# Latent attention: probabilities scaled before the transpose and split in two parts, values applied to two query tiles at once, residual rows parked in memory

## The chip, the cores and the metric

One core of a Trainium2 chip runs the whole program. The metric is the device time of one execution in microseconds; a profiled execution gives the trace.

## What is computed

Two transformer layers on 1024 tokens of width 1024, with mixers, a state space model, MLPs and, in the second layer, causal latent attention. The change is in that attention: 8 heads, query and key of 128 + 64 elements, values of 128.

```python
s = (q_nope @ k_nope.T + q_rope @ k_rope.T) * SM_SCALE      # per head, 1024 x 1024, float32
p = softmax(where(key <= query, s, -1e30))
o = p @ v                                                  # v = latent @ w, 128 wide
x = x + concat(o) @ w_o                                    # then layer norm and MLP
```

## The kernel before

Matrices that need float32 accuracy are held as a high and a low part of a shorter float format (`F32R`, a `Pair`); `mm3` multiplies such pairs with three instructions. Five engines run queues of their own, in an order written out by hand, tied by semaphores: TensorE (PE, `pe`) multiplies and transposes, VectorE (DVE, `dve`), ScalarE (ACT, `act`) and GpSimd (POOL) calculate, SyncE (SP) issues DMAs. TensorE writes PSUM, eight banks of 128x512.

`stage_attention` loops over heads `h`. A head starts with projections: `rope` in two halves, `nope`, `folded`, and in even heads `value_tiles`, which projects the values of two heads in four banks; `value_copy` brings them to SBUF in full float32. Then comes a loop over eight query tiles `t` of 128 rows. Tile `t` has `t+1` blocks of 128 keys (causal). In round `t` TensorE transposes the tile's exponentials (L3557), computes `scores` of tile `t+2` (in rounds 6 and 7 `keys` of the next head, in the last head `product.begin`, the first steps of the output product), transposes the finished rows of tile `t-1` (`turn_rows`, L3523) and multiplies the transposed exponentials with the values (L3580, full float32, two instructions a block). VectorE takes the maximum (L3665) and its negative (L3667), the reciprocal of the sum (L3701), scales the result rows (`scaled_rows`, L3672), copies part of the transposed exponentials (L3704) and makes the low part of the result (`low_part`, L3678). ScalarE makes exponentials with their sum (`expo`, L3608), copies the other part (L3626) and the high part of the result (L3613). The scaling by 1/sum stands behind the product with the values.

The order of VectorE in round `t`:

```python
if t: scaled_rows(h, t - 1)
# reciprocal(t); copy of blocks 4.. of tile t
if t + 2 < NT: maximum(h, t + 2)
if t == 0: rope_low(h, 1)
if t: low_part(h, t - 1)
```

Behind attention `Product` multiplies with the output weights: two passes over eight tiles at 256 columns, one at 512. Its weights come in four chunks over one raw buffer: SP loads chunk n when n-1 is split, GpSimd splits it (L289, L294). Chunk 1 may load once all heads are done. VectorE adds each result to the residual rows `x` (L1471), which lie in SBUF at 64 to 96 KB per partition throughout. TensorE's second pass waits for chunk 1's split and for the additions of the first.

## Time and profile before

| | us |
|---|---|
| median of 3 runs | 3170.9 (3167.88 to 3170.93) |
| the profiled execution | 3169.23, span 3167.4 |
| busy in the span: PE, DVE, ACT, POOL | 3096.3, 2017.4, 1063.0, 1410.4 |
| mean granted TensorE clock | 0.995 of full |
| attention stage, about | 2055 to 2395 |

Busy times are sums over the span; PE's matmuls overlap, so that its pace is read from their starts. A round's order on each engine is read from the timeline, and who waits for whom from the list of waits.

### The profile page before, as it was taken

What the parts mean: (1) busy time and instruction counts of PE and PEld (TensorE: products, weight loads), DVE (VectorE), ACT (ScalarE), POOL (GpSimd) and SP (SyncE); (2) the same over time, 40 slices, a digit from 0 to 9 for tenths busy, and PEclk for the clock granted to TensorE, in tenths of its full rate; (3) what the DMA queues carried; (4) which work ended last, traced back from release to release, by engine and by line L of the source; (5) the groups of instructions that cost most, each with busy time, mean ns of one, the idle gap of its engine ahead of it and who ended that gap; (6) DMA issues with size and microseconds to landing.
All of it is one profiled execution on the core that took longest, in us unless ns stands there. A gap on an engine that the chain in (4) does not pass through costs nothing.

```text
span 3167.4 us, 48769 instructions
## 1 busy us (share of the span) xinstructions
PE 3096.3 (98%) x17764; PEld 2629.3 (83%) x17764; DVE 2017.4 (64%) x3766; ACT 1063.0 (34%) x2061; POOL 1410.4 (45%) x1203
## 2 busy tenths in 40 slices
PE   9999999999999999999999999999999999999998
PEld 8787778788987889888888888988889788888886
DVE  4757576655898212777777775555553777777766
ACT  3546464631133210422222222544341422222221
POOL 5534343326544324755555545311114755555533
PEclk9999999999999999999999999999999999999999
DMA  7211111052212112011111111000002011111111
GB/s 204 75 53 53 53 53 52 14 203 82 71 29 57 53 53 94 27 54 53 46 46 53 53 40 64 11 17 18 17 21 94 28 53 53 53 53 53 53 53 53
DMA packets 181816, 179.39 MB, mean 57 GB/s; under 512 B 50234, under 2 KB 163066, under 8 KB 181498
## 3 DMA queue, kind: packets, MB, share of 16 engines
q1 hardware_dynamic: 181566, 177.02, 17.5%
q8 instruction: 104, 1.70, 0.2%
q14 instruction: 50, 0.41, 0.0%
q10 hardware_dynamic: 96, 0.26, 0.0%
HBM read 160.12 MB, written 22.38 MB: 58 GB/s over the span
## 4 chain that ended last, share of the span: by engine, by line
PE 63%; DVE 2%; issue 1%; ACT 1%; POOL 0%; POOLq 0%; DVEq 0%; ACTq 0%
PE banks L2763 17%; PE banks L79 14%; PE banks L81 14%; PE banks L80 14%; PE banks L3580 2%; PE banks L3557 1%; PE banks L215 1%; PE banks L3514 0%; PE banks L3515 0%; PE banks L3496 0%; POOL x L183 0%; PE banks L3523 0%; PE banks L2385 0%; DVE x L3000 0%; POOL rstd L178 0%
## 5 line engine op out<-in xcount | busy, mean ns | idle before, releaser
L3000 DVE TENSOR_TENSOR x<-x,banks 128x512 f32<-128x512 f32 x784 | 523.2, 687 | 241.4 <-PE banks L2763 232.9
L79 PE MATMUL banks<-winhi,xt_hi 128*128 128x512 f32 (+1 forms) x576 | 224.5, 390 | 8.4 <-ACT vz L990 3.8
L81 PE MATMUL banks<-winhi,xt_lo 128*128 128x512 f32 (+1 forms) x576 | 212.3, 369 | 0.0
L80 PE MATMUL banks<-winlo,xt_hi 128*128 128x512 f32 (+1 forms) x576 | 211.9, 368 | 0.0
L79 PE MATMUL banks<-h1t_hi,f1w_buf_hi 128*128 128x512 f32 x512 | 199.5, 390 | 1.6 <-issue 1.6
L79 PE MATMUL banks<-h3t_hi,f2w_buf_hi 128*128 128x512 f32 x512 | 199.5, 390 | 1.6 <-issue 1.6
L81 PE MATMUL banks<-h1t_hi,f1w_buf_lo 128*128 128x512 f32 x512 | 199.2, 389 | 0.0
L81 PE MATMUL banks<-h3t_hi,f2w_buf_lo 128*128 128x512 f32 x512 | 199.2, 389 | 0.0
L80 PE MATMUL banks<-h1t_lo,f1w_buf_hi 128*128 128x512 f32 x512 | 199.2, 389 | 0.0
L80 PE MATMUL banks<-h3t_lo,f2w_buf_hi 128*128 128x512 f32 x512 | 199.2, 389 | 0.0
L1013 ACT ACTIVATE scores<-scores,mixsmall 128x1024 f32<-128x1024 f32 (+2 forms) x128 | 122.8, 960 | 90.6 <-DVE mixsmall L1189 90.4
L633 POOL TENSOR_TENSOR mixsmall<-mixsmall,neghalf 128x4 f32<-128x4 f32 x64 | 66.3, 1035 | 190.2 <-DVE mixsmall L1152 190.1
L79 PEld LDWEIGHTS banks<-winhi,xt_hi 128*128 128x128 f32 x576 | 109.3, 190 | 43.9 <-issue 16.5
L81 PEld LDWEIGHTS banks<-winhi,xt_lo 128*128 128x128 f32 x576 | 109.2, 190 | 18.6
L80 PEld LDWEIGHTS banks<-winlo,xt_hi 128*128 128x128 f32 x576 | 109.5, 190 | 14.2
L79 PEld LDWEIGHTS banks<-h3t_hi,f2w_buf_hi 128*128 128x128 f32 x512 | 96.1, 188 | 21.7 <-issue 1.8
L79 PEld LDWEIGHTS banks<-h1t_hi,f1w_buf_hi 128*128 128x128 f32 x512 | 96.1, 188 | 21.6 <-issue 1.8
L81 PEld LDWEIGHTS banks<-h1t_hi,f1w_buf_lo 128*128 128x128 f32 x512 | 96.1, 188 | 20.0
L81 PEld LDWEIGHTS banks<-h3t_hi,f2w_buf_lo 128*128 128x128 f32 x512 | 96.1, 188 | 20.0
L80 PEld LDWEIGHTS banks<-h1t_lo,f1w_buf_hi 128*128 128x128 f32 x512 | 96.1, 188 | 19.9
L80 PEld LDWEIGHTS banks<-h3t_lo,f2w_buf_hi 128*128 128x128 f32 x512 | 96.1, 188 | 19.9
L2565 POOL TENSOR_TENSOR f1w_terms_lo<-f1w_raw,f1w_terms_hi 128x512 fp32r<-128x512 f32 x42 | 54.9, 1309 | 126.7 <-ACT f1w_terms_hi L2561 125.1
(552 smaller groups left out, 9327.2 us busy)
## 6 DMA issues: line engine op xcount, KB each, us to landing
f1w_raw<-in_w_ff SPq DMA_DIRECT2D x32, 1024.0 KB, 5.0
f2w_raw<-in_w_ff SPq DMA_DIRECT2D x32, 1024.0 KB, 5.1
winraw<-in_w_in SPq DMA_DIRECT2D x128, 128.0 KB, 2.4
gluw_raw<-in_ssm_w_glu SPq DMA_DIRECT2D x14, 512.0 KB, 4.6
x<-in_x SPq DMA_DIRECT2D x8, 512.0 KB, 6.4
wow_raw<-in_w_out SPq DMA_DIRECT2D x4, 1024.0 KB, 5.9
x<-in_x SPq DMA_DIRECT2D x1, 4096.0 KB, 14.8
gew_raw<-in_w_ple_gate SPq DMA_DIRECT2D x4, 1024.0 KB, 5.0
```

Source lines behind the costliest of these rows:

```text
L79: nc.tensor.matmul(out, a.hi, b.hi, start=start, stop=False)
L80: nc.tensor.matmul(out, a.hi, b.lo, start=False, stop=False)
L81: return nc.tensor.matmul(out, a.lo, b.hi, start=False, stop=stop)
L215: last = self.nc.tensor.transpose(self.bank(j, q)[:, k * P:(k + 1) * P], self.x[:, j, (4 * q + k) * P:(4 * q + k + 1) * P], self.chip.iden ...
L633: nc.gpsimd.tensor_tensor(m.rq[:, a % 2, :], m.ss4[:, a % 2, :], chip.neghalf[:, 0:1].to_broadcast([P, 4]), ALU.pow).then_inc(s_rp, 1)
L1013: nc.scalar.activation(m.s[:, g % 2, c, 0:w], m.s[:, g % 2, c, 0:w], ACT.Exp, bias=m.mx[:, g % 2, c:c + 1], accum_out=m.z[:, g % 2, c:c + ...
L2565: self.nc.gpsimd.tensor_tensor(self.terms.lo[:, k, :], self.source(k), f32(self.terms.hi[:, k, :]), ALU.subtract).then_inc(self.split, 1)
L2763: last = nc.tensor.matmul(chip.ps[:, 4 + 2 * (p % 2) + g, :], left, right, start=i == 0 and p in (0, 1, 3), stop=i == 2, skip_group_check= ...
L3000: nc.vector.tensor_tensor(xx, xx, chip.ps[:, 4 + 2 * (p % 2) + g, :], ALU.add).then_inc(s_acc, 1)
L3557: last = nc.tensor.transpose(chip.ps[:, 4 + n // 4, (n % 4) * P:(n % 4 + 1) * P], s[:, t % 2, n * P:(n + 1) * P], chip.ident[:, :])
L3580: last = nc.tensor.matmul(chip.ps[:, 6 + t % 2, 0:P], pt[:, t % 2, n * P:(n + 1) * P], v[:, n, h % 2, :], start=n == 0, stop=n == t)
```

## The change

Rows of exponentials are scaled by 1/sum in place in SBUF (`scaled_rows`, which now holds the reciprocal too) before TensorE transposes them (`turn`), in pieces of up to four blocks. ScalarE copies each piece as the high part (`turned_high`), VectorE subtracts for the low part (`turned_low`). The transposed parts of two tiles lie side by side in `pt`, and `pair_values` multiplies them with values that are split as well (`value_high`, `value_low`), with three instructions a block at 256 columns, half a pair in a round; pair 3 of a head is done within the next head, in its rounds 0 and 1 if the head before was even, between the two `rope` halves if it was odd, and behind `product.begin(pe, 2)` after the last. Its result comes out already transposed, so `turn_rows` goes; `pair_high` and `pair_low` split it. `pt` grows to 28 KB and takes the place of residual rows 0 to 6, which SP stores to memory when they are final and loads back at the end: rows 0 to 2 once pair 2 of the last head is done, 3 to 6 after pair 3, ahead of the output weights' chunk 1.

```diff
         self.nc, self.chip, self.ws, self.rows, self.x, self.x_scale, self.norm = nc, chip, ws, rows, x, x_scale, norm
-        self.ready, self.begun = ready, 0
+        self.ready, self.begun, self.rows_back = ready, 0, [None] * NT
...
             n, j = u // NT, u % NT
+            if n == 0 and self.rows_back[j] is not None:
+                dve.wait_ge(*self.rows_back[j])
...
-def stage_attention(nc, block, chip, io, latent, heads, ot, product):
+def stage_attention(nc, block, chip, io, latent, heads, ot, product, x, x_norm):
...
     with ExitStack() as ctx:
...
         qrt = chip.at("qrt", 32, [P, SEQ], F32R)
-        v = chip.at("v", 36, [P, NT, 2, VH])
+        v = Pair(chip.at("v_hi", 36, [P, NT, 2, VH], F32R), chip.at("v_lo", 52, [P, NT, 2, VH], F32R))
...
         s = chip.at("s", 44, [P, 2, SEQ])
-        pt = chip.at("pt", 52, [P, 2, SEQ])
+        pt = chip.at("pt", 64, [P, 14, 2, 2 * P], F32R)
+        AWAY, FREE = 7, 3
...
         ident_r = chip.at("ident_r", 61.5, [P, P], F32R)
-        rows = chip.at("rows", 62, [P, 2, VH])
...
-        def turned_rows(t):
-            return chip.ps[:, 6 + t % 2, P:2 * P].rearrange("p (c r) -> p c r", r=NT)
         VALUE_BANK = (6, 7, 1, 3)
-        def pair_of_tiles(n):
-            return v[:, 2 * n:2 * n + 2, :, :].rearrange("p t a n -> p (t a n)")
+        PAIRS_OF = NT // 2
+        FIRST_BLOCK = (0, 6, 0, 6)
+        PIECES = 12
+        def pieces(t):
+            if t < 4:
+                return [((4, 6, 5, 4)[t], 0, t + 1)]
+            return [(5, 0, 4), (4, 4, t + 1)]
+        def piece_at(h, t):
+            return PIECES * h + (t if t < 4 else 2 * t - 4)
+        def piece_bank(piece):
+            bank, first, last = piece
+            return chip.ps[:, bank, 0:(last - first) * P].rearrange("p (b q) -> p b q", q=P)
+        def piece_of(part, t, piece):
+            first = FIRST_BLOCK[t // 2]
+            return pt[:, first + piece[1]:first + piece[2], part, t % 2 * P:t % 2 * P + P]
+        def pair_rows(o, h, p):
+            return o[:, h:h + 1, :].rearrange("p a (r c) -> p (a c) r", r=NT)[:, 2 * p * (P // NT):2 * (p + 1) * (P // NT), :]
+        def pair_bank(p):
+            return chip.ps[:, 6 + p % 2, 0:2 * P]
+        def pair_of_tiles(z, n):
+            return z[:, 2 * n:2 * n + 2, :, :].rearrange("p t a n -> p (t a n)")
+        def ended_pair(h, t):
+            if t == 2:
+                return (h - 1, 3) if h % 2 else None
+            return (h, t // 2 - 2) if t in (4, 6) else None
...
         def _(sp):
+            for j in range(AWAY):
+                sp.wait_ge(x_norm.again, j + 1)
+                sp.dma_start(io["s_yt"][j, 0], x[:, j, :]).then_inc(s_away, 16)
...
             product.ws.load(sp, 0, first=True)
+            sp.wait_ge(s_away, 16 * AWAY)
+            sp.wait_ge(s_o, PAIRS_OF * N_HEADS - 1)
+            for j in range(FREE):
+                sp.dma_start(x[:, j, :], io["s_yt"][j, 0]).then_inc(s_home, 16)
+            sp.wait_ge(s_o, PAIRS_OF * N_HEADS)
+            for j in range(FREE, AWAY):
+                sp.dma_start(x[:, j, :], io["s_yt"][j, 0]).then_inc(s_home_2, 16)
...
         def _(pe):
-            pe.sem_inc(s_ol, NT)
...
-            def turn_rows(h, t):
-                pe.wait_ge(s_rows, h * NT + t + 1)
-                nc.tensor.transpose(chip.ps[:, 6 + t % 2, P:2 * P], rows[:, t % 2, :], chip.ident[:, :]).then_inc(s_ot, 1)
+            def turn(h, t):
+                pe.wait_ge(s_nr, h * NT + t + 1)
+                for n, (bank, first, last_block) in enumerate(pieces(t)):
+                    if t == 1:
+                        pe.wait_ge(s_vd, PAIRS_OF * (h // 2) + 1)
+                        if h:
+                            pe.wait_ge(s_ol, PAIRS_OF * h - 1)
+                    elif t == 2:
+                        pe.wait_ge(s_rl, 2 * h + 2)
+                    elif t == 3:
+                        pe.wait_ge(s_td, piece_at(h, 0) + 1)
+                    elif t == 4:
+                        pe.wait_ge(s_td, piece_at(h, 2 + n) + 1)
+                    elif t > 4:
+                        pe.wait_ge(s_td, piece_at(h, t - 1) + n + 1)
+                    for b in range(first, last_block):
+                        at = (b - first) * P
+                        last = nc.tensor.transpose(chip.ps[:, bank, at:at + P], s[:, t % 2, b * P:(b + 1) * P],
+                                                   chip.ident[:, :])
+                    last.then_inc(s_t, 1)
+            def pair_values(h, p, part):
+                if part == 0:
+                    pe.wait_ge(s_td, piece_at(h, 2 * p + 1) + len(pieces(2 * p + 1)))
+                    pe.wait_ge(s_vd, PAIRS_OF * (h // 2) + p + 1)
+                    if PAIRS_OF * h + p >= 2:
+                        pe.wait_ge(s_ol, PAIRS_OF * h + p - 1)
+                for b in range((p + 1) * part, (p + 1) * (part + 1)):
+                    q = P if b == 2 * p + 1 else 0
+                    w = Pair(v.hi[:, b, h % 2, :], v.lo[:, b, h % 2, :])
+                    rows = Pair(*(pt[:, FIRST_BLOCK[p] + b, half, q:2 * P] for half in range(2)))
+                    last = mm3(nc, pair_bank(p)[:, q:2 * P], w, rows, b == 0, b == 2 * p + 1)
+                if part:
+                    last.then_inc(s_o, 1)
...
             for h in range(N_HEADS):
+                if h:
+                    pe.wait_ge(s_td, PIECES * h)
                 rope(h, 0)
-                if h:
-                    turn_rows(h - 1, NT - 1)
+                if h and h % 2 == 0:
+                    pair_values(h - 1, 3, 0)
+                    pair_values(h - 1, 3, 1)
...
                 if h % 2 == 0:
-                    pe.wait_ge(s_ol, h * NT + NT)
+                    if h:
+                        pe.wait_ge(s_ol, PAIRS_OF * h)
...
                 for t in range(NT):
-                    pe.wait_ge(s_ex, h * NT + t + 1)
-                    for n in range(t + 1):
-                        last = nc.tensor.transpose(chip.ps[:, 4 + n // 4, (n % 4) * P:(n % 4 + 1) * P],
-                                                   s[:, t % 2, n * P:(n + 1) * P], chip.ident[:, :])
-                    last.then_inc(s_t, 1)
+                    turn(h, t)
...
                         product.begin(pe, t + 2 - NT)
-                    if t:
-                        turn_rows(h, t - 1)
-                    if t < 2:
-                        pe.wait_ge(s_vd, 4 * (h // 2) + 2)
-                    pe.wait_ge(s_ol, h * NT + (t + 7))
-                    pe.wait_ge(s_ta, h * NT + t + 1)
-                    if t >= 4:
-                        pe.wait_ge(s_td, h * 4 + t - 3)
-                    for n in range(t + 1):
-                        last = nc.tensor.matmul(chip.ps[:, 6 + t % 2, 0:P], pt[:, t % 2, n * P:(n + 1) * P], v[:, n, h % 2, :],
-                                                start=n == 0, stop=n == t)
-                    last.then_inc(s_o, 1)
+                    if t >= 2:
+                        pair_values(h, t // 2 - 1, t % 2)
+                    elif h % 2:
+                        pair_values(h - 1, 3, t)
             product.begin(pe, 2)
-            turn_rows(N_HEADS - 1, NT - 1)
+            pair_values(N_HEADS - 1, 3, 0)
+            pair_values(N_HEADS - 1, 3, 1)
...
-            def high_part(h, t):
-                act.wait_ge(s_ot, h * NT + t + 1)
-                nc.scalar.activation(token_rows(ot.hi, h, t), turned_rows(t), ACT.Copy).then_inc(s_oh, 1)
+            def turned_high(h, t):
+                if h == 0 and t == 0:
+                    act.wait_ge(s_away, 16 * AWAY)
+                elif t % 2 == 0 and h * PAIRS_OF + t // 2 >= 1:
+                    act.wait_ge(s_o, h * PAIRS_OF + t // 2 - 1)
+                for n, piece in enumerate(pieces(t)):
+                    act.wait_ge(s_t, piece_at(h, t) + n + 1)
+                    nc.scalar.activation(piece_of(0, t, piece), piece_bank(piece), ACT.Copy).then_inc(s_ta, 1)
+            def value_high(p, n):
+                act.wait_ge(s_v, 4 * p + n + 1)
+                nc.scalar.activation(pair_of_tiles(v.hi, n), chip.ps[:, VALUE_BANK[n], :], ACT.Copy).then_inc(s_vh, 1)
+            def pair_high(h, p):
+                act.wait_ge(s_o, h * PAIRS_OF + p + 1)
+                nc.scalar.activation(pair_rows(ot.hi, h, p), pair_bank(p).rearrange("p (c r) -> p c r", r=NT),
+                                     ACT.Copy).then_inc(s_oh, 1)
...
             for h in range(N_HEADS):
+                if h and h % 2 == 0:
+                    pair_high(h - 1, 3)
...
                 nope_high(h, 1)
+                if h % 2 == 0:
+                    value_high(h // 2, 0)
+                    value_high(h // 2, 1)
...
                 rope_high(h, 1)
+                if h % 2 == 0:
+                    value_high(h // 2, 2)
+                    value_high(h // 2, 3)
                 for t in range(NT):
-                    w = min(t + 1, 4) * P
-                    act.wait_ge(s_t, h * NT + t + 1)
-                    nc.scalar.activation(pt[:, t % 2, 0:w], chip.ps[:, 4, 0:w], ACT.Copy).then_inc(s_ta, 1)
-                    if t:
-                        high_part(h, t - 1)
+                    turned_high(h, t)
+                    ended = ended_pair(h, t)
+                    if ended is not None:
+                        pair_high(*ended)
...
                     key_high(h + 1)
-                high_part(h, NT - 1)
+                pair_high(h, 2)
+            pair_high(N_HEADS - 1, 3)
...
-            def value_copy(p, n):
-                dve.wait_ge(s_v, 4 * p + n + 1)
-                nc.vector.tensor_copy(pair_of_tiles(n), chip.ps[:, VALUE_BANK[n], :]).then_inc(s_vd, 1)
+            def value_low(p, n):
+                dve.wait_ge(s_vh, 4 * p + n + 1)
+                nc.vector.tensor_tensor(pair_of_tiles(v.lo, n), chip.ps[:, VALUE_BANK[n], :], f32(pair_of_tiles(v.hi, n)),
+                                        ALU.subtract).then_inc(s_vd, 1)
...
             def scaled_rows(h, t):
+                dve.wait_ge(s_ex, h * NT + t + 1)
+                nc.vector.reciprocal(inv[:, t % 2:t % 2 + 1], z[:, t % 2:t % 2 + 1]).then_inc(s_inv, 1)
                 dve.wait_ge(s_inv, h * NT + t + 1)
-                dve.wait_ge(s_o, h * NT + t + 1)
-                nc.vector.tensor_scalar(rows[:, t % 2, :], chip.ps[:, 6 + t % 2, 0:P], inv[:, t % 2:t % 2 + 1], None,
-                                        ALU.mult).then_inc(s_rows, 1)
-            def low_part(h, t):
-                dve.wait_ge(s_oh, h * NT + t + 1)
-                hi, lo = (token_rows(o, h, t) for o in (ot.hi, ot.lo))
-                nc.vector.tensor_tensor(lo, turned_rows(t), f32(hi), ALU.subtract).then_inc(s_ol, 1)
+                rows = s[:, t % 2, 0:(t + 1) * P]
+                nc.vector.tensor_scalar(rows, rows, inv[:, t % 2:t % 2 + 1], None, ALU.mult).then_inc(s_nr, 1)
+            def turned_low(h, t):
+                for n, piece in enumerate(pieces(t)):
+                    dve.wait_ge(s_ta, piece_at(h, t) + n + 1)
+                    nc.vector.tensor_tensor(piece_of(1, t, piece), piece_bank(piece), f32(piece_of(0, t, piece)),
+                                            ALU.subtract).then_inc(s_td, 1)
+            def pair_low(h, p):
+                dve.wait_ge(s_oh, h * PAIRS_OF + p + 1)
+                hi, lo = (pair_rows(o, h, p) for o in (ot.hi, ot.lo))
+                nc.vector.tensor_tensor(lo, pair_bank(p).rearrange("p (c r) -> p c r", r=NT), f32(hi),
+                                        ALU.subtract).then_inc(s_ol, 1)
...
                 if h:
-                    low_part(h - 1, NT - 1)
+                    pair_low(h - 1, 2)
+                if h and h % 2 == 0:
+                    pair_low(h - 1, 3)
...
                 if h % 2 == 0:
-                    value_copy(h // 2, 0)
-                    value_copy(h // 2, 1)
+                    value_low(h // 2, 0)
+                    value_low(h // 2, 1)
...
                 if h % 2 == 0:
-                    value_copy(h // 2, 2)
-                    value_copy(h // 2, 3)
+                    value_low(h // 2, 2)
+                    value_low(h // 2, 3)
+                scaled_rows(h, 0)
                 for t in range(NT):
-                    if t:
-                        scaled_rows(h, t - 1)
-                    dve.wait_ge(s_ex, h * NT + t + 1)
-                    nc.vector.reciprocal(inv[:, t % 2:t % 2 + 1], z[:, t % 2:t % 2 + 1]).then_inc(s_inv, 1)
-                    if t >= 4:
-                        dve.wait_ge(s_t, h * NT + t + 1)
-                        nc.vector.tensor_copy(pt[:, t % 2, HALF:(t + 1) * P], chip.ps[:, 5, 0:(t - 3) * P]).then_inc(s_td, 1)
+                    if t + 1 < NT:
+                        scaled_rows(h, t + 1)
+                    turned_low(h, t)
...
                         rope_low(h, 1)
-                    if t:
-                        low_part(h, t - 1)
-                scaled_rows(h, NT - 1)
+                    ended = ended_pair(h, t)
+                    if ended is not None:
+                        pair_low(*ended)
...
                     key_low(h + 1)
-            low_part(N_HEADS - 1, NT - 1)
-        done = [(s_ol, NT * N_HEADS + NT)]
-        return Ready([(s_o, NT * N_HEADS)], [(s_sc, NT * N_HEADS)], done, done)
+            pair_low(N_HEADS - 1, 2)
+            pair_low(N_HEADS - 1, 3)
+        product.rows_back = [(s_home, 16 * FREE)] * FREE + [(s_home_2, 16 * (AWAY - FREE))] * (AWAY - FREE) + [None]
+        done = [(s_ol, PAIRS_OF * N_HEADS)]
+        return Ready([(s_o, PAIRS_OF * N_HEADS)], [(s_sc, NT * N_HEADS)], done, done)
...
         latent, heads = Latents(nc, chip, io, after), HeadWeights(nc, chip, io)
+        rows_norm = normed("n7", "ln_ffn", 0, dst=after, banks=(0, 1, 4, 5))
         stage_mlp(nc, block, chip, "f1", product, io["w_ff1_2"][0], io["w_ff2_2"][0], ht, x, (96, 104, 120), (136, 144, 160),
-                  normed("n7", "ln_ffn", 0, dst=after, banks=(0, 1, 4, 5)), latent=latent, heads=heads)
+                  rows_norm, latent=latent, heads=heads)
...
         product = Product(nc, chip, "ao", ao, ot, x, 1.0, normed("n11", "ln_mix", 1, dst=ht), None)
-        product.ready = stage_attention(nc, block, chip, io, latent, heads, ot, product)
+        product.ready = stage_attention(nc, block, chip, io, latent, heads, ot, product, x, rows_norm)
```

## Rows read from the trace of the kernel before

**Rows 1.** The page, part 1: busy us (share of the span) xinstructions.

```profile
PE 3096.3 (98%) x17764; PEld 2629.3 (83%) x17764; DVE 2017.4 (64%) x3766; ACT 1063.0 (34%) x2061; POOL 1410.4 (45%) x1203
```

**Rows 2.** Waits, 2055 to 2400 us: total us, times, longest.

```profile
DVE mx L3665 <- PE banks L3518: 58.4, 44, 1.9
...
ACT s L3608 <- DVE mx L3667: 52.1, 56, 3.4
```

**Rows 3.** Timeline, PE, end of head 2: start us, us, instruction.

```profile
2187.57 1.95 PE L3580 MATMUL banks<-v,pt 128*128 128x128 f32 x16
...
2189.28 0.48 PE L79 MATMUL banks<-cqt_hi,qwp_hi 128*128 128x512 f32 x1
```

**Rows 4.** Timeline, PE, output product.

```profile
2395.28 0.36 PE L79 MATMUL banks<-aow_span,ot_hi 128*128 128x256 f32 x1
...
2410.83 0.28 PE L79 MATMUL banks<-aow_buf_hi,ot_hi 128*128 128x256 f32 x1
```

**Rows 5.** Groups by form, DVE, 2055 to 2400 us: xcount, busy us, mean ns, idle before.

```profile
L3704 DVE COPY pt<-banks 128x512 f32<-128x512 f32 x8 | 5.5, 692 | 3.0 <-PE banks L3557 3.0
...
L3704 DVE COPY pt<-banks 128x128 f32<-128x128 f32 x8 | 2.2, 271 | 0.0
```

**Rows 6.** Groups by form, ACT, 2055 to 2400 us.

```profile
L3626 ACT ACTIVATE pt<-banks 128x512 f32<-128x512 f32 x40 | 23.6, 590 | 16.4 <-PE banks L3557 16.4
```

**Rows 7.** In-place scaling of the mixer stage: timeline, and all instructions of its line.

```profile
327.07 0.96 DVE L1206 TENSOR_SCALAR scores<-scores,mixsmall 128x512 f32<-128x512 f32 x2
...
L1206 DVE TENSOR_SCALAR scores<-scores,mixsmall x64: 475/547/1559, 167.9 to 685.8; 128x512 f32<-128x512 f32 x32, 128x640 f32<-128x640 f32 x32
```

**Rows 8.** Timeline of head 3, tiles 3, 4 and 7, and the next head's start.

```profile
2205.85 0.19 ACT L3608 ACTIVATION_READ_ACCUMULATOR s<-banks,mx 128x1 f32 x1
...
2207.20 0.82 DVE L3665 TENSOR_REDUCE mx<-banks 128x1 f32<-128x640 f32 x1 [1.35 <-PE banks L3518]
...
2208.94 0.19 ACT L3608 ACTIVATION_READ_ACCUMULATOR s<-banks,mx 128x1 f32 x1
...
2218.16 1.22 DVE L3665 TENSOR_REDUCE mx<-banks 128x1 f32<-128x1024 f32 x1 [1.94 <-PE banks L3518]
...
2220.09 0.48 PE L79 MATMUL banks<-ckvt_hi,kwp_hi 128*128 128x512 f32 x1
...
2220.62 0.19 ACT L3608 ACTIVATION_READ_ACCUMULATOR s<-banks,mx 128x1 f32 x1
...
2221.57 0.27 PE L3523 MATMUL banks<-ident,rows 128*128 128x128 f32 x1
...
2227.31 0.48 PE L79 MATMUL banks<-cqt_hi,qwp_hi 128*128 128x512 f32 x1
```

**Rows 9.** Timeline of head 2: turn(0), last value copy, exp(3).

```profile
2163.08 0.27 PE L3557 MATMUL banks<-ident,s 128*128 128x128 f32 x1
...
2163.28 0.69 DVE L3661 COPY v<-banks 128x512 f32<-128x512 f32 x1 [0.75 <-PE banks L81]
...
2167.66 0.19 ACT L3608 ACTIVATION_READ_ACCUMULATOR s<-banks,mx 128x1 f32 x1
```

**Rows 10.** Timeline, SP and POOL, output product.

```profile
2392.92 0.37 SPq L265 DMA_DIRECT2D aow_raw<-in_attn_w_o  x1
...
2401.32 5.05 POOL L294 TENSOR_TENSOR aow_buf_lo<-aow_raw,aow_buf_hi 128x512 fp32r<-128x512 f32 x4
...
2425.65 5.05 POOL L294 TENSOR_TENSOR aow_span<-aow_raw,aow_span 128x512 fp32r<-128x512 f32 x4
```

**Rows 11.** DMA, 640 to 720 us in 40 slices; issues of the whole run: us to landing.

```profile
GB/s 0 0 73 352 407 410 424 426 424 418 414 303 404 156 14 242 528 459 344 508 418 131 0 0 0 0 8 0 0 0 190 340 142 90 66 240 277 226 376 193
...
aow_raw<-in_attn_w_o SPq DMA_DIRECT2D x4, 1024.0 KB, 5.0
```

**Rows 12.** Windows at the end: busy us of each engine, PEclk, DMA share, GB/s.

```profile
3152.00:3156.00 4.00, 2.84 (x13) 2.02 (x11) 3.90 (x8) 1.31 (x2) 2.93 (x2) 1.00 0.27 113
...
3156.00:3160.00 4.00, 0.00 (x0) 0.00 (x0) 3.90 (x8) 1.15 (x1) 4.00 (x3) 0.81 0.19 76
```

8 lines of the change are left out of this document (4 added, 4 removed).

## Prediction

> **What bounds the kernel now.** I read the page first: the matmul engine is busy for 98% of the span [rows 1], so a microsecond taken off it anywhere, or put on it as a pause, is a microsecond of the time, unless another engine becomes the one that is late. Then the waits of the attention stage, 2055 to 2400 us. They say who is ahead: VectorE waits 58.4 us for scores, ScalarE 52.1 us for VectorE's maximum [rows 2]; the matmul engine hardly stands in that list. So the stage runs at the pace of its matmuls, and the softmax steps arrive just ahead of them. Last the timelines of one odd head (3) and one even head (2), which give the slack of each hand-off.
>
> **Matmul work removed and added.** Each head's 36 blocks of probabilities times values are full f32, two instructions a block: 16 of them go from 2187.57 to 2189.28, 0.107 us each [rows 3]. 8 x 72 x 0.107 = 61.6 us go. So do 64 transposes of result rows, at about the same pace: 6.8 us. In their place stand 20 blocks a head of three instructions, 16 blocks at 256 columns and 4 at 128. The output product has that 256-column kind: from 2395.28 to 2410.83 it does 7x3 + 4x3 + 4x24 = 129 of them, 0.1205 each [rows 4]. For 128 columns I take 0.11, between the 0.107 above and this 0.1205; the two ends are 1 us apart over the kernel. 384 x 0.1205 + 96 x 0.11 = 56.9. The transposes of the probabilities and the value projections stay as many. Sum: 11.5 us less matmul work. If nothing else were late, that would be the result.
>
> **What VectorE and ScalarE get.** Per head VectorE loses eight row scalings, eight subtractions of 128 columns and four copies of 0.27 to 0.69 (0.135 + 0.14 per block of 128) [rows 5]. It gains eight in-place scalings of whole rows, twelve subtractions with the copy's costs (two operands, one in PSUM; 6.6 us), and four of 256 columns (about 2). That is some 5 us more in a head of 40, of which it now uses half: no lack of time. ScalarE gets four copies more of at most 0.59 [rows 6]. But the order matters. In the old order VectorE's maximum of tile t+2 waits only for scores. In the new one VectorE does scaled_rows(t+1), which waits for exp(t+1); then turned_low(t); then maximum(t+2), from which ScalarE makes exp(t+2), for which the next scaled_rows waits. These are now one closed chain, one step a tile, beside the matmuls and not before them. And turn(t+1) can't reuse its bank before turned_low(t).
>
> **Price of the scaling.** Nearest row: the same in-place scaling of f32 rows, 128x512, takes 0.96 for two, and 0.475 at least over all 64 [rows 7]. I take S = 0.41 at 384 columns, 0.48 at 512, and 0.07 more for each 128. The other end is the copy's slope, 0.14 for each 128 [rows 5]: S is 0.69 at 512 and 1.25 at 1024. The Trainium skill, "VectorE: DVE Perf Modes", the tier table, gives f32 tensor_scalar in SBUF twice the rate of tensor_tensor; the 0.475 agrees, the 1.56 us maximum in the same row doesn't. By the table the sum stays as below; at single rate it is 13 us more, as the rival says.
>
> **The chain, step by step.** E(x) is when the sum of exp(x) is read. From the start of the maximum to E: 2207.20 to 2209.13 is 1.93 for tile 4, 2218.16 to 2220.81 is 2.65 for tile 7, so 2.17 and 2.41 between, 1.69 for tile 3 [rows 8]. After E(x): reciprocal and two hand-offs 0.22, S(x), less 0.07 of overlap, then turned_low(x-1) (paced 0.50 for three blocks, 0.63 for four, then 0.21 or 0.35 for the rest), then that 1.93 to 2.65 for tile x+1. Steps: 3 to 4: 3.06; 4 to 5: 3.50; 5 to 6: 4.02; 6 to 7: 4.47; sum 15.05. After E(7) the first piece of turned_low(6) ends 1.60 later, the second 2.10; turn(7) ends 2.55 after E(7); then six instructions of keys, 1.48 as from 2220.09 to 2221.57 [rows 8], and the half pair, 1.05: the next head begins 5.08 after E(7). So E(3) to the next head is 20.1 us. Before, it was 2206.04 to 2227.31 = 21.27 in the odd head [rows 8] and 2167.85 to 2189.28 = 21.43 in the even one [rows 9, 3]. From turn(3), 0.76 behind E(3), that leaves 19.3 us, in which the matmuls fill some 16: 25 transposes 2.7, scores(5) to (7) 6.5 at 0.23 for 512 columns and 0.12 for 256, keys 3.0, five half pairs 4. The matmul engine pauses ahead of turn(4) to turn(7) for some 3 us a head, and only 1.1 and 1.3 are won on before. And pair 3, 24 instructions or 2.86 us, has been moved out of this stretch to where it costs its full time.
>
> **Even heads.** turn(0) started at 2163.08, right behind the value projections; the last value copy started at 2163.28 [rows 9]. Now ScalarE copies first (0.59), VectorE subtracts (0.69), both ahead of scaled_rows(0) in VectorE's queue, then 0.22 and 0.23 for it: turn(0) at 2165.03, 1.95 late. What is late next is scores(2), exp(2), and by the chain exp(3): 2.54 late at E(3). Add pair 3 of the head before, between the two rope projections (2.86), less its old transpose (0.12), less 1.30: +4.0 for heads 2, 4, 6; head 0 has no pair before it: +1.2.
>
> **Odd heads.** Pair 3 of the head before lies in two halves behind scores(2) and scores(3). It covers the first waits, but pushes scores(3): the 1.43 of the first half and 0.4 of the later turn(0), less the old product and its gaps, give E(3) 1.39 late; the second half pushes scores(4) 0.74 past its chain time. Less 1.14 and 0.12: +0.87. In head 7 begin() instead of keys costs 1.05 more, which now falls into a pause: -0.2. Behind it pair 3 of head 7 stands open: +2.9 less 0.1. Attention: 3x4.0 + 1.2 + 3x0.87 - 0.2 + 2.8 = 18.4 us slower.
>
> **The residual rows.** SP stores rows 0 to 6 as their rescaling ends, ahead of the first value load; the queue is idle there and the first use of pt is late: nothing. Coming back, three rows start begin(2) and a pair (2.5 + 2.9 us) before the end, four (2.1 MB) at the last s_o, and the first weight chunk, issued at 2392.92 [rows 10], now queues behind them. Reads from this same scratch ran at about 420 GB/s [rows 11]: 5.0 us later. (At the weights' own 1 MB in 5.0 us [rows 11] it would be 10; below, 0, if they don't delay each other.) GpSimd finished splitting that chunk 13.45 after the issue, at 2406.37, and the fourth at 2430.70, 37.8 after. Before, begin(2) and begin(3) lay behind the last s_o; now only begin(3): the second quarter of the product begins 15.55 after it. 13.45 + 5.0 - 15.55 = 2.9 of pause. The quarter takes 192 x 0.12 = 23.1, to 41.55; the fourth split is there at 42.8: 1.25 more. Together 4.2 us.
>
> **Sum.** 18.4 + 4.2 = 22.6 on the profiled execution's 3169.2 (span 3167.4) is 3191.8, forecast 3192. The median of the runs shown is 3170.9, 1.7 above that execution; 0.2% is about what a measurement of this kernel can tell from no change.
>
> **Rivals.** (a) The matmul engine still sets the pace, the side of faster. It decides if a step of the chain is shorter than the matmuls of its tile, for instance from 4 to 5 under 3.0 us instead of 3.50; for it speaks that VectorE now waits so long for scores [rows 2], against it that the scaling and the subtraction come to stand in front of each next maximum. Price: -11.5 + 4.2, 3162. Chance 0.10. (b) The scaling runs at single rate. For it speaks the mean of 538 ns and longest of 1559 in the mixer stage [rows 7], against it that GpSimd, busy there, has little to do here. S(3) to S(7) grow by 0.2 to 0.5, 1.65 a head: +13, 3205. Chance 0.13. (c) The rows come home unnoticed, the change's cover holds: -4.2, 3188. For it speaks that other loads overlapped; against, that all go in one queue. Chance 0.13. (d) The 2.9 us pause lets the matmul clock fall. After the last matmuls (2.84 us busy in a stretch of 4 at 1.00) the next 4 us, idle, show 0.81, a part of them at the level of 1.2 GHz [rows 12]. If some 4 us behind the pause ran at half pace, +2 to +3, 3195. Chance 0.08. The Trainium skill, "TensorE: Matmul & The Clock Gate", HAM oscillation, warns of just such gaps behind DMA waits; these rows agree that idleness lowers it, but no row here shows a pause of 3 us doing so. (e) Half of the pauses fill with work that I have put behind them, 3175 or less: chance 0.06, counted within 0.2%. The forecast itself has 0.50.
>
> **Numbers.** Low end: the chain 1 us a head shorter and no delay of the chunk, 3192 - 8 - 4, rounded down for the value copies to 3177; high end: single rate and the clock, 3207. Outside are (a), (e) and mixtures of (b) with (d) above: 0.19. Faster by over 0.2%: 0.10; within: 0.06; slower: 0.84.
>
> **What would show it.** VectorE's scaling of 1024 columns near 0.76 us. Maxima that start behind turned_low and not behind scores in tiles 5 to 7. Idle time of the matmul engine ahead of the transposes in turn(5), turn(6) and turn(7), 0.5 to 1.5 us each, and near 1.95 ahead of turn(0) in even heads. An odd head that lasts 38.9 us from rope to rope instead of 38.0, an even one 4 us longer than before. A pause of 3 us where the second quarter of the output product begins, and a GpSimd that waits for its chunk 5 us longer. The forecast is wrong if VectorE still waits for scores in most tiles, or if the 256-column instructions are issued further apart than 0.12 us.

## The result and the profile after

The changed kernel is slower: 3196.7 us median of 6 runs (3193.9 to 3204.5), beside 3170.8 for the kernel before in the same session; ratio 1.0086, 95% interval 1.0077 to 1.0096. The profiled execution took 3196.95 us, span 3195.1: 27.7 more span than before.

The page's first part, as [rows 1]:

```profile
PE 3095.7 (97%) x17604; PEld 2622.6 (82%) x17604; DVE 2066.1 (65%) x3798; ACT 1077.3 (34%) x2077; POOL 1410.2 (44%) x1203
```

The totals hardly moved; they hide it. One window over heads 0 to 6 (start of `rope(h, 0)` in head 0 to that in head 7), of the kernel before and then of the changed one (us, busy us of each engine and instructions, clock, DMA share, GB/s):

```profile
2064.52:2352.35 287.83, 286.34 (x1844) 252.63 (x1843) 148.69 (x378) 116.50 (x267) 31.90 (x34) 1.00 0.07 16
```

```profile
2066.93:2369.62 302.69, 278.82 (x1681) 240.76 (x1680) 189.43 (x408) 129.78 (x282) 31.90 (x34) 0.99 0.06 16
```

TensorE's work did fall, by 7.5 us. Its idle time rose from 1.5 to 23.9 us, and the stretch grew by 14.9. The waits of the changed kernel's attention, 2055 to 2425 us, say who is late now, as [rows 2]:

```profile
ACT s L3672 <- DVE mx L3754: 96.2, 55, 2.4
...
DVE inv_z L3758 <- ACT s L3672: 36.0, 40, 1.3
PEld banks L3578 <- DVE s L3761: 27.8, 25, 2.0
...
PE banks L3578 <- DVE s L3761: 12.9, 15, 1.8
...
PE banks L3578 <- DVE pt L3766: 11.0, 16, 1.1
...
DVE mx L3752 <- PE banks L3558: 4.7, 13, 0.6
```

VectorE waited 58.4 us for scores and now 4.7; it waits for the exponential instead, the exponential waits for the maximum, and TensorE's transposes (L3578) wait for both VectorE steps, the scaling (L3761) and the low half (L3766: `turned_low`; the high half is ScalarE's copy, `turned_high`, L3682). The chain's pace is read from where ScalarE reads the sum of each exponential ("the sum of tile t" from here on; a step is the time from one to the next): tiles 3 to 7 of head 2 in the changed kernel.

```profile
2177.29 0.19 ACT L3672 ACTIVATION_READ_ACCUMULATOR s<-banks,mx 128x1 f32 x1
...
2180.31 0.19 ACT L3672 ACTIVATION_READ_ACCUMULATOR s<-banks,mx 128x1 f32 x1
...
2183.78 0.19 ACT L3672 ACTIVATION_READ_ACCUMULATOR s<-banks,mx 128x1 f32 x1
...
2187.75 0.19 ACT L3672 ACTIVATION_READ_ACCUMULATOR s<-banks,mx 128x1 f32 x1
...
2192.16 0.19 ACT L3672 ACTIVATION_READ_ACCUMULATOR s<-banks,mx 128x1 f32 x1
```

The steps are 3.02, 3.47, 3.97 and 4.41 us, 14.87 in all. From the last row's end to the next head is 5.02 (2197.37). In the same head of the kernel before, where the matmuls set the pace, the steps were 3.25, 3.30, 3.89 and 4.48, 14.92 in all (sums at 2167.66 and 2182.58). So the chain is no slower than the matmuls were; but it does not get faster when TensorE's work in these tiles is taken away, and what was moved out of them (pair 3, the split of the values) costs its own time. The end of a round, VectorE in tile 7 of that head, has the loop in three rows: idle until the exponential, the scaling (0.76 for 1024 columns), then the low half.

```profile
2192.38 0.17 DVE L3758 RECIPROCAL inv_z<-z 128x1 f32<-128x1 f32 x1 [1.27 <-ACT s L3672]
2192.58 0.76 DVE L3761 TENSOR_SCALAR s<-s,inv_z 128x1024 f32<-128x1024 f32 x1
2193.25 1.15 DVE L3766 TENSOR_TENSOR pt<-banks,pt 128x512 fp32r<-128x512 f32 x2
```

The output product in the changed kernel, SP, GpSimd and TensorE, as [rows 10, 4], and two windows behind TensorE's first pause:

```profile
2415.00 1.95 SPq L3496 DMA_DIRECT2D x<-mixed_transposed  x4
2417.05 16.90 SPq L265 DMA_DIRECT2D aow_raw<-in_attn_w_o  x2
...
2426.59 1.90 POOL L289 CAST aow_buf_hi<-aow_raw 128x2048 fp32r<-128x2048 f32 x1 [35.38 <-DMA aow_raw<-in_attn_w_o]
2428.57 4.98 POOL L294 TENSOR_TENSOR aow_buf_lo<-aow_raw,aow_buf_hi 128x512 fp32r<-128x512 f32 x4
...
2433.60 0.39 PE L79 MATMUL banks<-aow_buf_hi,ot_hi 128*128 128x256 f32 x1 [3.12 <-POOL aow_buf_lo L294]
...
2454.46 5.01 POOL L294 TENSOR_TENSOR aow_span<-aow_raw,aow_span 128x512 fp32r<-128x512 f32 x4
...
2459.53 0.50 PE L79 MATMUL banks<-aow_span,ot_hi 128*128 128x512 f32 x1 [1.14 <-POOL aow_span L294]
```

```profile
2434.00:2436.00 2.00, 2.00 (x11) 2.00 (x11) 0.00 (x0) 0.00 (x0) 0.00 (x0) 0.50 0.68 174
2436.00:2438.00 2.00, 2.00 (x14) 2.00 (x14) 0.00 (x0) 0.00 (x0) 0.00 (x0) 0.67 0.97 336
```

The weights' second chunk stands behind the residual rows on SP's queue, its split is late, TensorE pauses for 3.12 us, and behind the pause the granted clock is at 0.50 and 0.67 of full, so wholly and then partly at 1.2 GHz, where it had been at 2.4. The quarter ends with a second pause, of 1.14 us, for the split of the fourth chunk.

Where the 27.7 us of span are, by stretches between the same instructions in both traces: ahead of attention +2.4 (unchanged code); head 0 +1.17; heads 2, 4, 6 +3.87, +3.85, +4.05; heads 1, 3, 5 +0.64, +0.63, +0.65; head 7 to the second quarter of the output product +5.50; that quarter +2.89 (25.93 for 23.04); the last pass of the product, behind it, +2.0.

### The profile page after: what moved, and what is told of

Read it like the earlier page. It is cut to its first block, busy times and chain, and to the rows that moved or that the text cites. A ratio compares the mean times of both kernels' runs of the same rounds, so it can differ in the third digit from the quotient of the medians.

```text
span 3195.1 us, 48516 instructions
## 1 busy us (share of the span) xinstructions
PE 3095.7 (97%) x17604; PEld 2622.6 (82%) x17604; DVE 2066.1 (65%) x3798; ACT 1077.3 (34%) x2077; POOL 1410.2 (44%) x1203
## 4 chain that ended last, share of the span: by engine, by line
PE 57%; DVE 5%; issue 1%; ACT 1%; POOL 1%; DMA 1%; SPq 0%; POOLq 0%; DVEq 0%; ACTq 0%
PE banks L2765 17%; PE banks L79 13%; PE banks L81 13%; PE banks L80 13%; DVE mx L3752 1%; DVE s L3761 1%; DVE pt L3766 1%; DMA aow_raw<-in_attn_w_o 1%; ACT s L3672 1%; PE banks L215 1%; PE banks L3578 0%; POOL x L183 0%; PE banks L3536 0%; DMA shift<-in_ln_mix_b 0%; POOL aow_span L294 0%
```

## The experiments

Each is an edit of the changed kernel unless it says otherwise. "Changed" is the 3196.7 above; the kernel before took 3169.2 to 3171.1 beside them.

### e1: the low half first

```diff
-                    if t + 1 < NT:
-                        scaled_rows(h, t + 1)
                     turned_low(h, t)
+                    if t + 1 < NT:
+                        scaled_rows(h, t + 1)
```

> VectorE takes the subtraction of the low half of a tile's transposes ahead of the scaling of the next tile's rows; in the changed kernel it was the other way round. The closed chain (theory): in tiles 3 to 7 the scaling of the next tile stands between the transposes and the low half for which the next transposes wait, and VectorE waits there for the exponential. With the low half first, the longest steps from one row sum to the next fall from 3.97 to about 3.6 us (5 to 6) and from 4.40 to about 3.7 us (6 to 7), and the last transposes of a head come about 1 us earlier: about 2 us for each of 8 heads, 16 us in all, 3181 us. VectorE's amount of work as the bound (rival): the same instructions in another order change nothing, 3197 us within 3. TensorE's own work as the bound (rival): 3197 us as well. It could also lose: TensorE's next transposes wait for rows that are scaled later; if that wait ends last, steps 3 to 4 grow by the low half's 0.29 to 0.42 us, and the time rises by up to 6 us.

3221.8 us, 25 slower than changed: neither theory's number, and four times the loss that was allowed for. The steps from tile 4 to 7 in head 3 are 3.95, 4.46 and 4.90 us, each 0.5 longer than in the changed kernel. The waits, 2055 to 2425 us, name what I had overlooked:

```profile
DVE pt L3766 <- ACT pt L3682: 68.7, 62, 1.8
PEld banks L3578 <- DVE s L3761: 61.6, 55, 2.0
```

ScalarE copies the high half of tile t behind the exponential of t+1. The low half can't start before that copy, so VectorE stood idle through it, and the scaling came after; in the changed kernel the scaling fills this time. The closed chain has two strands: exponential, scaling; and exponential, high half. Both join in the low half, ahead of the maximum.

### e2: the scaling twice

```diff
-                nc.vector.tensor_scalar(rows, rows, inv[:, t % 2:t % 2 + 1], None, ALU.mult).then_inc(s_nr, 1)
+                nc.vector.tensor_scalar(rows, rows, inv[:, t % 2:t % 2 + 1], None, ALU.mult).then_inc(s_inv, 1)
+                dve.wait_ge(s_inv, 2 * (h * NT + t + 1))
+                nc.vector.tensor_scalar(rows, rows, 1.0, None, ALU.mult).then_inc(s_nr, 1)
```

> The scaling of the rows is followed by a second multiplication of the same rows by 1.0, so that its cost is there twice and the values stay what they are. Theory: the scaling lies on the chain of every head from the moment the exponential is done, with 0.49 to 0.75 us in tiles 3 to 7 (0.49, 0.55, 0.62, 0.69, 0.75: together 3.1 us a head), so that the time grows by about 25 us over 8 heads, and by up to 8 more from tiles 0 to 2 of a head (0.13, 0.29, 0.35: 0.77 us a head, 6 us in all): 3222 to 3228 us. Rival, TensorE or ScalarE sets the pace and VectorE has room (it is busy for about two thirds of this stage): under 6 us more, 3197 to 3203 us.

3228.4 us, 31.7 more, at the top of the theory's two terms (25 and 6). VectorE had room for the work by its busy share; it had none on the chain. A small part may be the clock: in heads 2, 4 and 6 of this run it is 0.66 in a stretch of 5 us (from 2180, 2272 and 2368), and heads 4 and 5 grew by 4.6 and 4.5 us where heads 2 and 3 grew by 3.6 and 4.0.

### e3: the residual rows behind the weights' second chunk

```diff
             self.ws.load(sp, n)
+            if n == 1 and self.behind_first is not None:
+                self.behind_first()
```

(`behind_first` holds the loads of rows 3 to 6.)

> Residual rows 3 to 6 are loaded back behind the second chunk of the output product's weights on SP's queue, not ahead of it; all else is as in the changed kernel. Theory: the chunk's split waits for its load, the load for the rows ahead of it, and TensorE pauses for 3.1 us at the chunk's first product; without the pause the granted clock stays at its upper level in the stretch behind it (another 1.6 us), so that the output product ends 4 to 5 us earlier; with what comes behind it, 3190 to 3193 us. The additions of the residual rows would then wait, if at all, for under 1 us. Rival, the chunk is late for another reason (POOL's cast and split of the chunk before it, or bandwidth in use by other loads): within 1 us of the changed kernel, 3196 us.

3187.2 us, 9.5 less (7.2 between the spans), more than was expected. The trace of this kernel has no pause: the cast begins 4.7 us behind its load's issue at 2415.96 (changed: 9.5 behind 2417.05), and the clock stays.

```profile
2420.68 1.89 POOL L289 CAST aow_buf_hi<-aow_raw 128x2048 fp32r<-128x2048 f32 x1 [29.32 <-DMA aow_raw<-in_attn_w_o]
...
2430.77 0.28 PE L79 MATMUL banks<-aow_buf_hi,ot_hi 128*128 128x256 f32 x1
```

```profile
2434.00:2438.00 4.00, 4.00 (x36) 4.00 (x35) 0.69 (x2) 0.00 (x0) 3.92 (x4) 1.00 0.00 0
```

From head 7 to the second quarter it gains 3.3 us, the quarter takes 23.04 again (2.9: the fourth chunk's split no longer makes TensorE wait), and 1.5 come in the last pass.

### e4: the first scaling ahead of the values

```diff
+                scaled_rows(h, 0)
                 if h % 2 == 0:
                     value_low(h // 2, 2)
                     value_low(h // 2, 3)
-                scaled_rows(h, 0)
```

> In the four even heads the rows of tile 0 are scaled ahead of the low halves of values 2 and 3, where the kernel before scaled them; in the changed kernel they come behind. Theory: TensorE's first transposes of an even head wait 1.8 us for the scaling; ahead of the values it would come up to 1.9 us earlier, but VectorE's maximum of tile 2 then follows the same two low halves as before and sets the next step, so that about 1 us of it is left at the end of the head: 4 us over four heads, 3192 to 3193 us. Rival, the whole delay of 1.9 us goes through to the end of the head: 7.6 us, 3189 us. Rival, the even heads are late for another reason (the values' own transposes): no change, 3197 us.

3192.5 us, 4.2 less, the number that was expected, but in part by luck: of 4.3 us between the spans 1.7 arose ahead of attention, heads 0, 2 and 4 gained 0.3 us each, not 1, and head 6 gained 1.4. At the sum of tile 2 all had gained 1.2. What took it back is one scaling, in head 2 here (VectorE, then GpSimd), which in head 6 takes 0.42:

```profile
2171.81 1.36 DVE L3761 TENSOR_SCALAR s<-s,inv_z 128x384 f32<-128x384 f32 x1
...
2343.31 0.42 DVE L3761 TENSOR_SCALAR s<-s,inv_z 128x384 f32<-128x384 f32 x1
```

```profile
2171.69 1.26 POOL L3392 TENSOR_TENSOR vwp_lo<-vw,vwp_hi 128x512 fp32r<-128x512 f32 x1
```

It ends at 2173.17, 0.22 behind GpSimd's 2172.95.

### e5: GpSimd held back

```diff
+            if gates is not None:
+                pool.wait_ge(*gates[n])
...
+                heads.do_split(pool, h, [(s_nr, scaled + 3), (s_nr, scaled + 5)])
                 if h % 2 and h + 1 < N_HEADS:
+                    pool.wait_ge(s_nr, scaled + 6)
```

(`scaled` is `NT * (h - 1)`; the rest as e4.)

> As e4_scale_before_values, and GpSimd holds its splits of the next head's weights back until the scalings of tiles 2, 4 and 5 of a head are done, so that none of them runs beside the scalings of tiles 0 to 2. In e4 seven of the eight heads show a scaling that lasts longer than elsewhere (128x384 1.29 to 1.36 us in heads 0, 2 and 4, against 0.42 in head 6), each of which ends about 0.22 us behind the end of a GpSimd instruction. Theory (an in-place scaling in SBUF doesn't start while a GpSimd instruction holds SBUF): these go back to 0.29 and 0.42 us, each of heads 0, 2 and 4 gets 0.9 us shorter, with the smaller ones 3 to 4 us in all against e4: 3188.5 to 3189.5 us. Rival (the long scalings come from the DMA that lands beside them or from the write port of the exponential): they stay as long, 3192 us.

3189.9 us, 2.6 less than e4; its four runs lie between 3182.9 and 3192.1, so the heads say more. Heads 0, 2 and 4 are shorter by 0.88, 0.92 and 0.90, the scaling of tile 2 takes 0.42 in each. The smaller delays were worth nothing: in odd heads TensorE's work reaches further than the 0.1 to 0.9 us that they cost.

### e6: GpSimd busy

```diff
+            for again in range(5 if h and n else 0):
+                self.nc.gpsimd.tensor_tensor(self.w[n].hi[:, :, :], self.raw[n][:, :, :], self.raw[n][:, :, :],
+                                             ALU.add).then_inc(self.again, 1)
+                pool.wait_ge(self.again, (h - 1) * 5 + again + 1)
```

> The changed kernel, in which GpSimd repeats five additions of two SBUF operands (1.84 us each, written where the cast comes behind them, so that the values stay) in each of heads 1 to 7 ahead of its own split; nobody waits for the result earlier than before. Theory (lock between the fast in-place scaling and GpSimd): three to four scalings a head fall into these 9 us, each waits on average half of 1.84 us, and all lie on the chain: 15 to 25 us more than the changed kernel, 3212 to 3222 us, with scalings of up to 2.3 us in the trace. Rival (no lock; GpSimd is off every path): within 2 us of the changed kernel, 3195 to 3199 us.

3203.2 us, 6.5 more (9.0 between the spans), between the two numbers expected: the lock is there, the price is about half of the least I gave. 24 scalings last up to 2.01 us, here three in head 1 that should take 0.42, 0.49 and 0.55:

```profile
2130.11 1.35 DVE L3765 TENSOR_SCALAR s<-s,inv_z 128x384 f32<-128x384 f32 x1
...
2133.76 0.87 DVE L3765 TENSOR_SCALAR s<-s,inv_z 128x512 f32<-128x512 f32 x1
...
2137.16 0.68 DVE L3765 TENSOR_SCALAR s<-s,inv_z 128x640 f32<-128x640 f32 x1
```

```profile
2129.78 7.72 POOL L3368 TENSOR_TENSOR qwp_hi<-qw 128x768 fp32r<-128x768 f32 x5
```

Odd heads grew by 0.3 to 0.4 us only, since the delays of tiles 2 and 3 end inside the matmuls of the half pairs there; heads 0, 2, 4 and 6 by 3.7, 1.9, 2.3 and 0.8. Not all of this is the lock's: in heads 0, 2 and 4 of this run the clock falls too (0.72 in 2085 to 2097 us, 0.66 in 2177 to 2182 and in 2266 to 2271), in head 6 it doesn't. How the growth of those three heads divides is not shown.

### e7 and e8: three edits together, and the last tile

e7 is e3 and e5 with the last two low halves of the values moved on:

```diff
                         rope_low(h, 1)
+                    if t < 2 and h % 2 == 0:
+                        value_low(h // 2, 2 + t)
```

> Three edits together: the residual rows behind the weights' second chunk (e3), GpSimd's splits held back (e5), and in even heads the low halves of values 2 and 3 moved into the rounds of tiles 0 and 1, behind the maxima of tiles 2 and 3 (e4 had them between the scalings of tiles 0 and 1). Theory: 9.5 us from e3, 3 to 4 from GpSimd, 2 to 3 for e4's part, and another 1 us for each even head since the scaling of tile 1 now comes 1.4 us earlier: 3176 to 3180 us. Rival (the gains lie on the same waits and don't add): 3184 us or more.

3181.1 us. The first two parts add within the scatter of e5's runs (e5 less e3's gain is 3180.4), but the later low halves brought 0.36 us an even head and not 1: the sum of tile 2 came 0.8 earlier, that of tile 3 only 0.35.

```diff
+                    if t == NT - 2:
+                        expo(h, NT - 1)
...
-                    if t + 2 < NT:
+                    if t + 3 < NT:
                         expo(h, t + 2)
...
-                    if t + 1 < NT:
+                    if t + 2 < NT:
                         scaled_rows(h, t + 1)
                     turned_low(h, t)
+                    if t + 2 == NT:
+                        scaled_rows(h, t + 1)
```

> As e7_combined, and in the last round but one ScalarE copies the high half of tile 6 ahead of the exponential of tile 7, VectorE takes its low half ahead of the scaling of tile 7, where VectorE waits 1.27 us for that exponential. Theory: the exponential of tile 7 begins 0.25 us later, but the transposes of tile 7 need only the scaling behind it: 0.5 us a head earlier, 4 us less than e7. Rival (as in e1, where low first made VectorE wait for ScalarE): ScalarE's order was changed with it here, but if the exponential is pushed by more than 0.7 us, the time is that of e7 or longer.

3176.9 us, 4.2 less: every head is 0.55 to 0.65 us shorter. Low first pays where ScalarE's high half goes first as well.

### e9, e11 and e10: one instruction less, with and without the chain

e9, and the same edit in the kernel before (e11), and in e8 (e10). Not shown here: the sign is turned in the scaling of the queries, in the mask and in the exponential.

```diff
-                nc.vector.reduce_max(mx[:, t % 2:t % 2 + 1], wide(t), axis=mybir.AxisListType.X).then_inc(s_mx, 1)
-                dve.wait_ge(s_mx, h * NT + t + 1)
-                nc.vector.tensor_scalar(mx[:, t % 2:t % 2 + 1], mx[:, t % 2:t % 2 + 1], -1.0, None, ALU.mult).then_inc(s_nm, 1)
+                nc.vector.tensor_reduce(mx[:, t % 2:t % 2 + 1], wide(t), axis=mybir.AxisListType.X, op=ALU.min).then_inc(s_nm, 1)
```

> The changed kernel with scores of the opposite sign (query parts scaled by -SM_SCALE, mask with the other sign): VectorE takes their minimum, which is the bias of the exponential as it stands, and the instruction that negated the maximum (0.15 us and a hand-off, 0.2 together) falls away in each of the 64 rounds; the probabilities stay what they are. Theory (closed chain exponential, scaling, low half, maximum, exponential): each of the steps from the sum of tile 3 to that of tile 7 gets 0.2 us shorter, less where the matmuls come next (step 5 to 6 has 0.3 us of room), and in even heads two steps before them: 0.6 to 1.1 us a head, 5 to 9 us in all, 3188 to 3192 us. Rival (the pace is that of the matmuls): under 1 us.

3185.6 us, 11.1 less (attention from head 0 to head 7: 7.1 less; 4.0 of the span's difference arose ahead of it). Sums of tiles 3, 4 and 7 in head 2:

```profile
2171.16 0.19 ACT L3672 ACTIVATION_READ_ACCUMULATOR s<-banks,mx 128x1 f32 x1
...
2173.99 0.19 ACT L3672 ACTIVATION_READ_ACCUMULATOR s<-banks,mx 128x1 f32 x1
...
2185.27 0.19 ACT L3672 ACTIVATION_READ_ACCUMULATOR s<-banks,mx 128x1 f32 x1
```

From tile 3 to 7 it is 14.11 us for 14.87: 0.19 for each of four steps, the whole price of the instruction and its hand-off. The room ahead of the matmuls was larger than I had put it.

> The same edit in the kernel before. Theory: there VectorE waits 58.4 us for scores, the maximum is no link of a closed chain, and the same 0.2 us a round are worth 0 to 2 us: 3169 to 3171 us. Rival (the softmax steps were as late in the kernel before): as much as in e9, 5 to 9 us less.

3167.9 us, ratio to the kernel before 0.9994 (0.9985 to 1.0003): not told from no change. Over heads 0 to 6 it is 1.9 us shorter than the kernel before (285.93 for 287.83), e9 7.1 shorter than the changed kernel (295.59 for 302.69). The same instruction is worth nearly four times as much on the closed chain. (e9's trace also settles a question on the output product, below.)

> All edits of e8_last_tile and e9_minimum together. Theory: e8 still has pauses of TensorE of some 2.5 us in an odd head and 4 in an even one, most of them ahead of the transposes of tiles 2 and 4 to 7, behind the chain: 0.6 to 1.1 us a head less than e8 (3176.9), 3168 to 3172 us, about the time of the kernel before. Rival (e8 took the same waits away already): 3175 us or more.

3170.8 us, ratio to the kernel before 1.0002 (0.9993 to 1.0011). All that the experiments found, put into the changed kernel, brings it back to where the kernel before stands, and no further; the kernel before with the same minimum (e11) is 2.9 us faster. Heads 0 to 6:

```profile
2059.43:2345.53 286.10, 275.33 (x1682) 239.27 (x1680) 180.20 (x352) 129.40 (x282) 32.33 (x34) 1.00 0.07 16
```

10.8 us of idle time are left of 23.9, and the stretch is 1.7 shorter than before; pair 3 behind the last head takes that back.

### e12: no scaling at all

```diff
-                pe.wait_ge(s_nr, h * NT + t + 1)
+                pe.wait_ge(s_ex, h * NT + t + 1)
```

(`scaled_rows` and its calls are gone.)

> The changed kernel without the reciprocal and the scaling of the rows, so that the probabilities aren't divided by their sum: the output is another, and only the time counts. They take 0.7 to 0.95 us a round on the chain in tiles 3 to 7. Theory, after e1: beside the chain through the scaling runs a second one, exponential of t+1, high half of tile t behind it on ScalarE, low half of t, maximum of t+2, exponential of t+2, only 0.2 to 0.35 us shorter. So the steps from sum to sum fall from 3.02, 3.47, 3.97 and 4.40 to about 2.75, 3.2, 3.7 and 4.05 us, VectorE waits for ScalarE's high halves in place of its exponentials, and with 1 to 2 us more for each head from tiles 0 to 2 it is 18 to 26 us less: 3171 to 3179 us. Rival (the scaling is the whole delay, its 0.9 us a round come back in full): the steps fall to those of the matmuls, about 4 us a head for tiles 3 to 7 alone and 5 to 6 in all, 3150 to 3160 us.

3176.0 us, 20.7 less than changed. The steps from tile 3 to 7 in head 2 are 2.82, 3.29, 3.73 and 4.10, and the waits, 2055 to 2425 us, have the second strand:

```profile
ACT s L3672 <- DVE mx L3754: 86.2, 55, 2.1
DVE pt L3759 <- ACT pt L3682: 67.9, 60, 1.8
```

Taking 0.7 to 0.95 us out of a step shortened it by 0.2 to 0.3. Even free of cost the scaling would leave this kernel slower than before as a whole. Where it is slower has changed, though: heads 0 to 6 take 284.18 us, 3.7 less than in the kernel before (287.83), with 10.7 us of TensorE's idle time; the output product, in which the residual rows still stand ahead of the second chunk, takes this back and more (+4.8 to its second quarter, +3.1 in it, +1.5 in the last pass, between the traces), and 2.8 arose ahead of attention. This edit together with e3's was not run.

## Why the prediction was right, and where its terms were off

The forecast was 3192 (3177 to 3207); 3196.7 was measured, and the reason was the one forecast: the pace passed from the matmuls to the chain through VectorE. Rival (a) falls with the idle 23.9 us and e9 against e11; (e) with them. (c) falls with e3.

That the number came so near is in part luck. Between the traces it is 27.7 us for 22.6. Attention was put too high (17.1 measured for 18.4: 14.9 in heads 0 to 6 and 2.2 from head 7 to the end of the product's first quarter), the pause and the quarter behind it too low (6.2 for 4.2), and 4.4 us lie in places where nothing was forecast.

**TensorE's work.** 11.5 us less over the kernel was the forecast. The trace shows 7.5 less busy time in seven heads; 7/8 of the forecast would be 10.1. The two aren't quite the same measure: busy time counts the end of a matmul ahead of each pause (a 256-column one is issued every 0.12 us and shown for 0.28), and TensorE has 38 idle stretches in these seven heads for 10. An estimate from these numbers, 28 x 0.16 = 4.5 us, is more than the missing 2.6; what share it has is not shown.

**The chain.** 3.06, 3.50, 4.02, 4.47 and 5.08 were forecast, 3.02, 3.47, 3.97, 4.41 and 5.02 measured in even heads: the rows of before were enough. In odd heads the first step is 3.78 (sums of tiles 3 and 4 of head 3 at 2215.19 and 2218.97), set by the matmuls, as forecast with 3.06 + 0.74. The pauses were put too high: ahead of turn(5), (6) and (7) 0.5 to 1.5 us each were forecast, 0.44, 0.13 and 1.06 are there in head 2; ahead of turn(4) to (7) together 1.9 in head 2 and 1.6 in head 3, for some 3. What the argument lacked was the second strand. It made no difference to the sum, since the scaling was the longer one, but e1's expectation failed by it.

**Heads.** Even +4.0 (3.87, 3.85, 4.05), head 0 +1.2 (1.17), the stretch from head 7 on +5.5 (5.50). Odd +0.87 was 0.64, a small error in two terms: the sum of tile 3 came 1.25 us late for 1.39, and the stretch from its end to the next head takes 20.65 for 20.87. The 5.50 of the last stretch is made of 2.2 for 2.6 up to the end of the first quarter, and 3.3 for 2.9 from there to the first matmul of the second (idle for 3.12 of it), so that it fits by two errors that cancel.

**turn(0) in even heads.** Forecast 1.95 late; the trace shows a wait of 1.80 there:

```profile
2171.98 0.33 PE L3578 MATMUL banks<-ident,s 128*128 128x128 f32 x1 [1.80 <-DVE s L3761]
```

An earlier scaling gave back 0.3 us a head in e4 and 1.2 in e5, once GpSimd was out of its way.

**Price of the scaling.** Forecast 0.41 at 384 and 0.07 for each 128: 0.42, 0.49, 0.55, 0.62, 0.69, 0.76. Rival (b), single rate, did not come as such. What it rested on, the long instructions of [rows 7], has its match here: the mean at 384 columns was 622 ns, and e4, e5 and e6 show the cause. An in-place scaling of f32 rows in SBUF that meets a GpSimd instruction ends 0.2 us behind it. In the changed kernel it happened in heads 1, 3, 5 and 7 at tile 2, 0.09 to 0.85 us each, and nearly all was hidden. I had written that GpSimd has little to do in this stage; it has 32 us, and they fall where the heads begin.

**The residual rows.** The forecast had the second chunk 5.0 us later. From SP's first issue behind the last pair to the chunk's cast it is 11.6 us (2415.00 to 2426.59), before 6.4 (2392.92 [rows 10] to 2399.34): 5.2. Pause 2.9, measured 3.12. The quarter behind: 1.25 forecast, 2.89 measured; e3 shows both gone together. The clock fell there as rival (d) has it, and the quarter's matmuls took 24.51 us from first to last for 22.92. But this is not where the 1.6 us come from: the quarter ends when the fourth chunk is split (2459.47, and TensorE goes on at 2459.53), so the slower matmuls only shortened the pause of 1.14 us ahead of it. e9 shows it, with a pause nearly as long at the quarter's start and no fall of the clock (1.00 from 2422 to 2446 us):

```profile
2421.37 0.39 PE L79 MATMUL banks<-aow_buf_hi,ot_hi 128*128 128x256 f32 x1 [2.90 <-POOL aow_buf_lo L294]
...
2446.46 0.50 PE L79 MATMUL banks<-aow_span,ot_hi 128*128 128x512 f32 x1 [1.79 <-POOL aow_span L294]
```

```profile
2422.00:2426.00 4.00, 4.00 (x35) 4.00 (x35) 0.42 (x1) 0.00 (x0) 0.00 (x0) 1.00 0.78 262
```

The quarter takes 25.09 us all the same, and the pause at its end is longer. The mis-sized term is the fourth split, taken as 5.0 us later like the second: from the second chunk's split to the fourth's it is 25.9 us for 24.3 before, since the third chunk's load took 6.7 us from issue to cast for 5.0 (5.7 in e9). Why that load is slower stays open.

**Not foreseen.** 2.0 us in the last pass of the product. In the changed kernel the next stage's loads (weights, gain, shift) are all issued within 1.6 us, 2459.5 to 2461.1, behind the late fourth split; VectorE waits 4.8 us for `shift`, and TensorE's transposes at 2477.91 wait 1.7 us for GpSimd's step behind it. In e3 VectorE waits 3.4, and 1.5 of the 2.0 are back. And 2.4 us ahead of attention, in code that the change doesn't touch. They arise between 600 and 680 us; in the first half of that stretch the clock differs:

```profile
600.00:640.00 40.00, 36.58 (x279) 32.41 (x277) 27.14 (x67) 22.05 (x46) 12.54 (x25) 1.00 0.00 1
```

```profile
600.00:640.00 40.00, 36.63 (x265) 31.74 (x264) 25.18 (x60) 20.10 (x41) 13.02 (x27) 0.96 0.00 1
```

(the kernel before, then the changed one). Kernels with this same code reach head 0 anywhere from 2059.4 to 2067.3 us, so it is scatter as far as the runs show; that the clock makes the difference is argued from these windows, and why it dips in one execution and not in the other stays open.

## What to carry to other kernels

Before work is taken off the busiest engine, write down for each hand-off which engine waits for which, and ask whether the change closes a loop among the others: a microsecond on such a loop counts once a round whatever the busy shares say, and shortening one strand shows only how long the next is. Order matters as a pair of queues: moving VectorE's low half first cost 25 us when it was done in all tiles and alone, and gained 4 in the last tile with ScalarE's copy moved too. A load put ahead of others on one queue makes all those behind it late, the last one that somebody waits for too. And before a fallen clock is given a price, see what the slower engine waits for next: here the slower matmuls ended in a pause that was there anyway.
